# The memory's running maxima by DRAM and GpSimd, a fifth bank for the second attention's heads, the inverse sums turned a step later

## The chip, the cores and the metric

The kernel runs on one core of a Trainium2 chip. A core has five engines with a queue of their own: TensorE (PE in the rows; PEld is its weight load), VectorE (DVE), ScalarE (ACT), GpSimd (POOL) and SyncE (SP), which issues most of the DMAs. They meet only in semaphores. PE writes its products to PSUM, which has eight banks of 128 partitions x 512 floats. The metric is the device time of one execution in microseconds (us); lower is better.

## The reference, cut to what matters

Three transformer layers on 512 tokens of width 1024. The change touches the mixer of the third, in which two things run side by side: an attention of 8 heads, and a memory with matrix state (an mLSTM) of 4 heads, run forwards and backwards.

```python
# attention of the third layer, per head
s = einsum('bkgqd,bksd->bkgqs', q_blk, kt) * scale
p = softmax(s, axis=-1)
o = einsum('bkgqs,bksd->bkgqd', p, vt)

# memory, per head, chunk by chunk
d = b[..., :, None] - b[..., None, :] + ic[..., None, :]
m_t = maximum(b + m[..., None], max(where(tril, d, -inf), axis=-1))
s = einsum('bhtd,bhsd->bhts', qc, kc) * exp(d - m_t[..., None])
num = w_inter[..., None] * einsum('bhvd,bhtd->bhtv', C, qc) + einsum('bhts,bhsv->bhtv', s, vc)
h = num / maximum(abs(den), exp(-m_t))[..., None]
```

The kernel doesn't chunk the memory. It computes for each head and direction the whole 512 x 512 triangle of weights exp(a[s] - M[t]), where a is a number for each key and M a running maximum for each query, taken from the first token on (direction 0) or from the last (direction 1).

## The kernel before

**The whole.** Weights come in chunks of up to 1 MB through three buffers `raw[:, 0..2]`; ACT rounds a chunk to its high half (`wh`, L1278), DVE makes the low half (`wl`, L1906), and every large product is three PE passes. SP's `fetch(i)` may overwrite a buffer of `raw` when the low half of chunk i-3 is made. `mixed[2]` is the number of the first of the four chunks of the third layer's output weights `w_out`; they are named here +0 to +3. `mixed[2] - 1` and +2 use `raw[:, 0]`, +0 and +3 use `raw[:, 1]`, +1 uses `raw[:, 2]`.

**The stage.** On each engine the order is that of the program text. Two generators, `attend("B", ...)` and `memory()`, are advanced in turn by `side_by_side`: one step of the heads, one of the memory. The heads' first two steps come earlier, among the jobs under the last product of the input projection.

Heads: 16 units u of a head pair (j = u // 4) and a query block, each with two scores i = 2u and 2u+1. In step u PE issues the two score products of u (L848, each shown as two instructions), the transposes of the two probabilities of u-2 (L857, eight), in every fourth step `turn_inverses(j)`, one transpose of the inverse sums of the pair (L883), and for odd u-4 the output of a pair and half the queries (L873). DVE scales the scores and takes their minimum of the negated values (L2148, into one of four buffers `pl`, so only when the transpose of score i-4 has read it), forms the inverse sums (L2155), copies every second transposed probability (L2163) and the turned inverse sums (L2171). ACT takes the exponential (L1436) and copies the other transposed probabilities (L1380 into `xf`). The turned inverse sums go through DRAM (`spread`, SP's L2900 and L2907) and reach all partitions; GpSimd multiplies the pair's output with them (L2855), `DIVIDED["B"]` = 4 steps later, and ACT and DVE (L2177) make its halves.

Memory: m = 0..7 is a head and a direction; each has four cells, one for each block t of 128 keys. `Mr[d]` holds the running maxima of four heads as four rows. For each m:
- `start(m)` on PE (L1160): a product with a column of the identity, which copies row `hh` of `Mr[d]` to all 128 partitions of bank 5 (`B_MAX`). It is issued at cell 2 of m-1.
- `own(m)` on DVE (L2592): `Dd = a - M` for the four diagonal blocks, at cell 3 of m-1; it waits for the last weighing of m-2, which has read the buffer.
- `masked(m)` on GpSimd (L2863): the triangle's other side is set to a large negative number.
- ACT: the exponential of the diagonal blocks (L1770), and `decay(m, t)`, the exponential of the blocks beside the diagonal, straight from bank 5 (L1763) into one of three buffers `Db`.
- PE: `score(m, t)` (L1168) and, one m later, `outcome(m, tt)` (L1182). DVE: `weigh(m, t)` multiplies the scores with the exponentials (L2607, L2610); `divide` (L2619 to L2632) finishes the outcome.

At cell 0 of m = 3 ACT and DVE also make chunk +1 (`cur.reach`): ACT's L1278, then DVE's L1906, in the midst of their lists.

**Banks.** `banks.take(name, hold, among)` takes the bank of those in `among` whose last use was given out longest ago, and the taker waits until the engine that reads the last user's value is done. The heads use banks 0 to 3 for scores, transposes and inverse sums (`B_UNITS`) and bank 4 for the output, `M` has bank 5, scores and outcomes of the memory 6 and 7, and all but 5 once the heads are through (`B_LATE`).

**Behind the stage.** PE multiplies the attention's half with +0 (`first_column(0)`, L1216), spreads two gates (L1229), transposes the memory's output (L1237), takes +1, and then +2 and +3 (L644 on). ACT makes the high halves of +2 and +3 directly after the memory's last step, before it copies the gates.

## Time and profile before

| | us |
|---|---|
| median of 3 runs | 1911.02 |
| lowest, highest | 1909.43, 1911.91 |
| the profiled execution | 1908.34 |
| its span | 1906.6 |
| PE busy | 1848.9 (97% of the span) |
| PEld busy | 1495.3 (78%) |
| DVE busy | 1151.6 (60%) |
| ACT busy | 734.6 (39%) |
| POOL busy | 108.8 (6%) |
| mean granted clock of PE | 0.994 |

The rows further down come from one profiled execution. Its own time is 1908.34 us, of which the span between the first and the last record is 1906.6 us, so 1.7 us lie around it. The granted clock is given as a share of full speed: 1.00 is 2.4 GHz, and the lower of the two levels, 1.2 GHz, is 0.5; a stretch's number is the mean over it. "Idle before" is the time in which an engine did nothing before an instruction, with what ended it. PE's instructions overlap, so the distance from start to start is what one of them costs, and not its length.

### The profile page before, as it was taken

Reading aid. Unit: us, or ns where it says so; the run is one execution under the profiler, and the core shown is the slowest. Engines: PE = TensorE matmul, PEld = TensorE weight load, DVE = VectorE, ACT = ScalarE, POOL = GpSimd, SP = SyncE. Lnnn points to the kernel's source line nnn. Section 1 sums busy time; section 2 is a strip of 40 time slices with the busy share of each in tenths; the row PEclk is TensorE's granted clock in tenths of the full one; section 3 lists DMA queues with packets and bytes.
Section 4 is the critical chain, followed back from the end, with each engine's and each line's share of the span. In section 5 each row is a group of like instructions: output and inputs, shape, how many; then the busy total and the mean of one; then the engine's idle time right before and its main releaser. Section 6 shows DMA issues by size and latency. Waiting matters only on the chain.

```text
span 1906.6 us, 22855 instructions
## 1 busy us (share of the span) xinstructions
PE 1848.9 (97%) x9156; PEld 1495.3 (78%) x9156; DVE 1151.6 (60%) x2038; ACT 734.6 (39%) x1155; POOL 108.8 (6%) x109
## 2 busy tenths in 40 slices
PE   9999999999999999999999999899988999999997
PEld 7775888878888888878888888688655798888885
DVE  4987676555557686567554544976666554333438
ACT  4458352233233434544322222365554352222221
POOL 0341000000000152000000000000001000000000
PEclk9999999999999999999999999999999999999999
DMA  6221425433432121233434343122100313223221
GB/s 207 67 72 35 161 89 173 158 133 133 149 138 91 62 72 45 66 133 107 137 112 131 111 132 111 46 90 88 67 17 28 100 34 121 89 95 104 89 89 45
DMA packets 119018, 187.24 MB, mean 98 GB/s; under 512 B 7664, under 2 KB 72400, under 8 KB 115840
## 3 DMA queue, kind: packets, MB, share of 16 engines
q1 hardware_dynamic: 117520, 180.96, 28.9%
q0 software_dynamic: 1392, 4.82, 0.8%
q8 instruction: 72, 1.18, 0.3%
q14 instruction: 34, 0.28, 0.0%
HBM read 183.62 MB, written 2.15 MB: 97 GB/s over the span
## 4 chain that ended last, share of the span: by engine, by line
PE 77%; DVE 15%; ACT 4%; issue 3%; DMA 1%; POOL 0%; DVEq 0%; SPq 0%; ACTq 0%; POOLq 0%
PE bank L622 10%; PE bank L624 10%; PE bank L623 10%; PE bank L815 7%; PE bank L813 7%; PE bank L814 7%; PE bank L596 2%; PE bank L598 2%; PE bank L597 2%; DVE wl L1906 2%; PE bank L873 2%; DVE gb L2259 2%; PE bank L848 2%; PE bank L857 2%; DVE m L2257 1%
## 5 line engine op out<-in xcount | busy, mean ns | idle before, releaser
L1906 DVE TENSOR_TENSOR wl<-raw,wh 128x2048 fp32r<-128x2048 f32 (+1 forms) x137 | 308.2, 2254 | 190.7 <-ACT wh L1278 190.1
L1278 ACT ACTIVATE wh<-raw 128x2048 fp32r<-128x2048 f32 (+1 forms) x142 | 265.1, 1882 | 227.9 <-PE bank L815 90.4
L622 PE MATMUL bank<-xh,wh 128*128 128x512 f32 (+1 forms) x872 | 343.0, 393 | 4.0 <-DVE wl L1906 4.0
L623 PE MATMUL bank<-xh,wl 128*128 128x512 f32 (+1 forms) x872 | 342.2, 392 | 0.0
L624 PE MATMUL bank<-xl,wh 128*128 128x512 f32 (+1 forms) x872 | 342.2, 392 | 0.0
L815 PE MATMUL bank<-wh,ul 128*128 128x512 f32 x592 | 230.5, 389 | 0.0
L814 PE MATMUL bank<-wl,uh 128*128 128x512 f32 x592 | 230.4, 389 | 0.0
L813 PE MATMUL bank<-wh,uh 128*128 128x512 f32 x592 | 230.4, 389 | 0.0
L622 PEld LDWEIGHTS bank<-xh,wh 128*128 128x128 f32 (+1 forms) x872 | 163.5, 187 | 43.2 <-DVE wl L1906 5.1
L624 PEld LDWEIGHTS bank<-xl,wh 128*128 128x128 f32 (+1 forms) x872 | 163.5, 187 | 37.4
L623 PEld LDWEIGHTS bank<-xh,wl 128*128 128x128 f32 (+1 forms) x872 | 163.5, 187 | 36.7
L596 PE MATMUL bank<-wh,xh 128*128 128x512 f32 (+1 forms) x352 | 138.3, 393 | 1.7 <-DVE wl L1906 1.7
L2073 DVE TENSOR_TENSOR h<-h,bank 128x512 f32<-128x512 f32 x112 | 75.4, 683 | 105.1 <-PE bank L815 102.1
L1400 ACT ACTIVATE A<-bank 128x512 f32<-128x512 f32 x64 | 38.2, 596 | 259.0 <-PE bank L624 255.4
L598 PE MATMUL bank<-wh,xl 128*128 128x512 f32 (+1 forms) x352 | 134.1, 381 | 0.0
L597 PE MATMUL bank<-wl,xh 128*128 128x512 f32 (+1 forms) x352 | 133.9, 380 | 0.0
L814 PEld LDWEIGHTS bank<-wl,uh 128*128 128x128 f32 x592 | 111.1, 188 | 23.3
L813 PEld LDWEIGHTS bank<-wh,uh 128*128 128x128 f32 x592 | 111.2, 188 | 23.2
L815 PEld LDWEIGHTS bank<-wh,ul 128*128 128x128 f32 x592 | 111.1, 188 | 23.2
L2082 DVE TENSOR_TENSOR A<-A 128x512 f32<-128x512 f32 x64 | 44.1, 689 | 93.7 <-ACT A L1400 93.4
L1380 ACT ACTIVATE A<-bank 128x512 f32<-128x512 f32 (+4 forms) x106 | 51.4, 489 | 88.8 <-PE bank L598 32.3
L596 PEld LDWEIGHTS bank<-wh,xh 128*128 128x128 f32 x352 | 66.2, 188 | 16.6 <-issue 2.6
(352 smaller groups left out, 2962.6 us busy)
## 6 DMA issues: line engine op xcount, KB each, us to landing
raw<-in_mlp_w_up SPq DMA_DIRECT2D x32, 1024.0 KB, 5.6
raw<-in_mlp_w_down SPq DMA_DIRECT2D x32, 1024.0 KB, 5.1
raw<-in_w_ada SPq DMA_DIRECT2D x24, 1024.0 KB, 5.0
raw<-in_b_w_in SPq DMA_DIRECT2D x12, 1024.0 KB, 5.3
raw<-in_w_gate SPq DMA_DIRECT2D x11, 1024.0 KB, 5.3
raw<-in_w_up SPq DMA_DIRECT2D x11, 1024.0 KB, 5.5
raw<-in_w_in SPq DMA_DIRECT2D x10, 1024.0 KB, 5.1
raw<-in_w_down SPq DMA_DIRECT2D x10, 1024.0 KB, 5.0
```

What stands on the lines that cost most here:

```text
L596: pe.matmul(o, X, H[:, k, :], start=kk == 0, stop=False)
L597: pe.matmul(o, X, L[:, k, :], start=False, stop=False)
L598: step = pe.matmul(o, Y, H[:, k, :], start=False, stop=kk == 7)
L622: pe.matmul(o, H[:, k, c], xh[:, k, :], start=k == 0, stop=False)
L623: pe.matmul(o, L[:, k, c], xh[:, k, :], start=False, stop=False)
L624: step = pe.matmul(o, H[:, k, c], xl[:, k, :], start=False, stop=k == 7)
L813: pe.matmul(o, X, H[:, f, :], start=f == 0, stop=False)
L814: pe.matmul(o, X, L[:, f, :], start=False, stop=False)
L815: step = pe.matmul(o, Y, H[:, f, :], start=False, stop=f == nf - 1)
L1278: act.activation(slots[slot_of[i]][0][:, 0:n], raw[:, i % NRAW, 0:n], ACT.Copy).then_inc(*s_high.up(i))
L1906: dve.tensor_tensor(L[:, 0:n], raw[:, i % NRAW, 0:n], H[:, 0:n].bitcast(F), ALU.subtract).then_inc(*s_low.up(i))
L2073: dve.tensor_tensor(hv, hv, ps, ALU.add).then_inc(*s_row.up(name))
```

## The change

- `start(m)` is gone, and with it `M`'s bank. SP writes `Mr[0]` and `Mr[1]` to a DRAM tensor `rows_m` and loads row (d, hh) from there to all 128 partitions of one of four buffers `Mb`, which lie in `raw[:, 0]`. The first four are loaded once the low half of chunk `mixed[2] - 1` is made, m = 4 + j behind the spreading of the inverse sums of pair j, when ACT and GpSimd have read m - 4.
- `raw[:, 0]` is thus taken until ACT and GpSimd have read the last maxima. Chunk +2 is fetched only then, and +3 and the chunks behind it after +2, in SP's order. Before, +2 was issued as soon as `raw[:, 0]` was free, ahead of the stage, and +3 at 1356.4 us.
- DVE's `own(m)` is gone. GpSimd subtracts M from a itself, directly ahead of the selection, at cell 2 of m-1 instead of 3, and waits there for the maxima's transfer and the last weighing of m-2.
- ACT's `decay` reads `Mb` and waits for the transfer, not for DVE.
- `B_UNITS` is (0, 1, 2, 3, 5). When the heads are through the memory takes any bank.
- `INVERTED = {"A": 0, "B": 1}`: the inverse sums of the heads "B" are transposed and copied one step later. The attention of the first layer ("A") stays as it is.

```diff
-        B_UNITS, B_OUT, B_MAX, B_MEM, B_LATE, ANY = range(4), (4,), (5,), (6, 7), (0, 1, 2, 3, 4, 6, 7), range(8)
+        B_UNITS, B_OUT, B_MEM, ANY = (0, 1, 2, 3, 5), (4,), (6, 7), range(8)
+        INVERTED = {"A": 0, "B": 1}
+        Mb = [raw[:, 0, 512 * i:512 * i + 512] for i in range(4)]
+        def maxima(m):
+            return s_maxima[m % 4], 16 * (m // 4 + 1)
+        def maxima_read(m):
+            return s_act.at(("Db", m, T - 2 if MEM[m][1] == 0 else T - 1))
...
-                        if g % T == T - 1:
-                            turn_inverses(g // T)
+                    g = u - lag - INVERTED[key]
+                    if 0 <= g < N and g % T == T - 1:
+                        turn_inverses(g // T)
...
-                def start(m):
-                    hh, d = MEM[m]
-                    b = banks.take(("M", m), False, B_MAX)
-                    sel = ident[32 * d:32 * d + 4, 32 * d + hh:32 * d + hh + 1].broadcast_to([4, P])
-                    w.wait_ge(*banks.free(("M", m), s_act.sem))
-                    w.wait_ge(*s_step.at(("Mr", d)))
-                    pe.matmul(bank[b][:, :], sel, Mr[d], start=True, stop=True).then_inc(*s_mm.up(("M", m)))
...
-                    w.wait_ge(*s_step.at(("D", m)))
+                    w.wait_ge(*maxima(m))
                     w.wait_ge(*s_act.at(("ecol", 1)))
-                    act.activation(Db[n % 3][:, 0:o1 - o0], bank[banks.of["M", m]][:, o0:o1], ACT.Exp, bias=acol[:, d, t, hh:hh + 1],
+                    act.activation(Db[n % 3][:, 0:o1 - o0], Mb[m % 4][:, o0:o1], ACT.Exp, bias=acol[:, d, t, hh:hh + 1],
...
-                def own(m):
-                    hh, d = MEM[m]
-                    M = bank[banks.of["M", m]][:, :].rearrange("p (t q) -> p t q", t=T)
-                    w.wait_ge(*s_mm.at(("M", m)))
-                    w.wait_ge(*s_act.at(("ecol", 1)))
-                    if m > 1:
-                        w.wait_ge(*s_step.at(("ST", m - 2, T - 1)))
-                    dve.scalar_tensor_tensor(Dd[m % 2], M, -1.0, acol[:, d, :, hh].unsqueeze(2).broadcast_to([P, T, P]), ALU.mult,
-                                             ALU.add).then_inc(*s_step.up(("D", m)))
...
-                    w.wait_ge(*s_step.at(("D", m)))
+                    hh, d = MEM[m]
+                    w.wait_ge(*maxima(m))
+                    w.wait_ge(*s_act.at(("ecol", 1)))
+                    w.wait_ge(*(s_step.at(("ST", m - 2, T - 1)) if m > 1 else s_step.at(("conv", 7))))
+                    pool.tensor_tensor(Dd[m % 2], acol[:, d, :, hh].unsqueeze(2).broadcast_to([P, T, P]),
+                                       Mb[m % 4].rearrange("p (t q) -> p t q", t=T), ALU.subtract).then_inc(*s_pool.up(("own", m)))
+                    w.wait_ge(*s_pool.at(("own", m)))
...
-                        if m + 1 < len(MEM) and t == 3:
+                        if m + 1 < len(MEM) and t == 2:
                             masked(m + 1)
...
+            def spread_maxima(m):
+                hh, d = MEM[m]
+                if m > 3:
+                    w.wait_ge(*maxima_read(m - 4))
+                    w.wait_ge(*s_pool.at(("own", m - 4)))
+                sp.dma_start(Mb[m % 4], rows_m[d, hh].partition_broadcast(P)).then_inc(s_maxima[m % 4], 16)
...
-                if i == mixed[2] + 3:
+                if i == mixed[2] + 1:
+                    for d in range(2):
+                        w.wait_ge(*s_step.at(("Mr", d)))
+                        sp.dma_start(rows_m[d], Mr[d]).then_inc(s_rows, 16)
+                    w.wait_ge(s_rows, 32)
+                    w.wait_ge(*low_of(mixed[2] - 1))
+                    for m in range(4):
+                        spread_maxima(m)
                     for j in range(4):
                         spread("B", j)
+                        spread_maxima(4 + j)
+                    w.wait_ge(*maxima_read(len(MEM) - 1))
+                    w.wait_ge(*s_pool.at(("own", len(MEM) - 1)))
```

**The order on PE, steps u = 5 and 6.** Before; the list begins in step 5 with the transposes (L857), and goes on with inverse sums, output, a product of the memory, the maxima of m = 1 and the scores of step 6:

```order
L857 MATMUL bank1<-C,pl 128x128 [waits s_step]
L857 MATMUL bank1<-C,pl 128x128 x3
L883 MATMUL bank3<-C,att 8x128 [waits s_step]
L873 MATMUL bank4<-xf,A 64x256 x8
L1168 MATMUL bank7<-A 128x256
L1160 MATMUL bank5<-A,C 128x512 [waits s_act]
L848 MATMUL bank0<-A 128x512 [waits s_act,s_step]
L848 MATMUL bank2<-A 128x512
```

Now (L872, L888, L1176, L863, L898 are the lines L857, L873, L1168, L848, L883 of before):

```order
L872 MATMUL bank3<-C,pl 128x128 [waits s_act]
L872 MATMUL bank3<-C,pl 128x128 x3
L888 MATMUL bank4<-xf,A 64x256 x8
L1176 MATMUL bank7<-A 128x256
L863 MATMUL bank5<-A 128x512 [waits s_step]
L863 MATMUL bank0<-A 128x512
L872 MATMUL bank2<-C,pl 128x128 [waits s_step]
L872 MATMUL bank2<-C,pl 128x128 x3
L872 MATMUL bank1<-C,pl 128x128 [waits s_act]
L872 MATMUL bank1<-C,pl 128x128 x3
L898 MATMUL bank3<-C,att 8x128 [waits s_step]
```

The maxima's product is gone, and the inverse sums stand behind the transposes of step 6, in a bank that no score of the step has.

**The order on PE, the last head pair, steps u = 16 to 18.** Before, from the last transposes on:

```order
L857 MATMUL bank0<-C,pl 128x128 x3
L857 MATMUL bank2<-C,pl 128x128 x4
L883 MATMUL bank1<-C,att 8x128 [waits s_step,s_act]
L873 MATMUL bank4<-xf,A 64x256 x8
L1168 MATMUL bank6<-A 128x384 [waits s_step]
L1182 MATMUL bank7<-A,xf 128x130 x7
L1160 MATMUL bank5<-A,C 128x512 [waits s_act]
```

Now:

```order
L872 MATMUL bank5<-C,pl 128x128 x3
L872 MATMUL bank0<-C,pl 128x128 [waits s_act]
L872 MATMUL bank0<-C,pl 128x128 x3
L888 MATMUL bank4<-xf,A 64x256 [waits s_act]
L888 MATMUL bank4<-xf,A 64x256 x7
L1176 MATMUL bank6<-A 128x384 [waits s_step]
L1190 MATMUL bank7<-A,xf 128x130 x7
L898 MATMUL bank2<-C,att 8x128
```

The output (L888, before L873) stands ahead of the inverse sums (L898, before L883), which come after the outcome of the memory (L1190, before L1182).

**The order on GpSimd, from the first maxima on.** Before, from the masks of m = 0 and 1 to that of m = 4 (L2855 is the heads' division, L2863 the selection):

```order
L2863 AFFINE_SELECT rz<-rz 128x512 [waits s_step] x2
L2855 TENSOR_TENSOR pl<-pl,A 128x512 [waits s_inv_b0,s_act]
L2863 AFFINE_SELECT rz<-rz 128x512 [waits s_step]
L2855 TENSOR_TENSOR pl<-pl,A 128x512 [waits s_inv_b1,s_act]
L2863 AFFINE_SELECT rz<-rz 128x512 [waits s_step]
L2855 TENSOR_TENSOR pl<-pl,A 128x512 [waits s_inv_b0,s_act]
L2863 AFFINE_SELECT rz<-rz 128x512 [waits s_step]
```

Now (L2847 is the division, L2857 the subtraction, L2860 the selection):

```order
L2857 TENSOR_TENSOR rz<-acol,raw 128x512 [waits s_step,s_act,s_maxima0]
L2860 AFFINE_SELECT rz<-rz 128x512 [waits s_pool]
L2857 TENSOR_TENSOR rz<-acol,raw 128x512 [waits s_maxima1]
L2860 AFFINE_SELECT rz<-rz 128x512 [waits s_pool]
L2847 TENSOR_TENSOR pl<-pl,A 128x512 [waits s_inv_b0,s_act]
L2857 TENSOR_TENSOR rz<-acol,raw 128x512 [waits s_step,s_maxima2]
L2860 AFFINE_SELECT rz<-rz 128x512 [waits s_pool]
L2847 TENSOR_TENSOR pl<-pl,A 128x512 [waits s_inv_b1,s_act]
L2857 TENSOR_TENSOR rz<-acol,raw 128x512 [waits s_step,s_maxima3]
L2860 AFFINE_SELECT rz<-rz 128x512 [waits s_pool]
```

Each selection has a subtraction ahead of it, which is what waits for the maxima's transfer and for DVE.

## Rows read from the trace of the kernel before

**Rows 1.** Windows: start:end, length, busy of each engine, granted clock, DMA share, GB/s
```profile
1366.00:1434.26 68.26, 60.44 (x360) 34.88 (x358) 42.15 (x120) 39.15 (x103) 6.36 (x7) 1.00 0.05 13
...
1438.33:1445.70 7.37, 7.37 (x33) 4.50 (x33) 3.65 (x12) 0.00 (x0) 0.00 (x0) 0.59 0.25 52
```

**Rows 2.** Groups by form, 1360 to 1485: shape, count, busy us, mean ns, idle
```profile
L1160 PE MATMUL bank<-A,C 4*128 4x512 f32 x16 | 9.0, 639 | 0.0
...
L2592 DVE SCALAR_TENSOR_TENSOR rz<-bank,acol 128x512 f32<-128x512 f32 x8 | 5.5, 684 | 3.0 <-PE bank L1160 3.0
...
L2855 POOL TENSOR_TENSOR pl<-pl,A 128x512 f32<-128x512 f32 x4 | 5.1, 1272 | 13.4 <-ACT pl L1380 13.4
...
L2863 POOL TENSOR_SCALAR_AFFINE_SELECT rz<-rz 128x512 f32<-128x512 f32 x8 | 5.1, 634 | 202.3 <-DVE rz L2592 202.3
...
L2607 DVE SCALAR_TENSOR_TENSOR xf<-bank,rz 128x384 f32<-128x384 f32 x4 | 2.2, 552 | 1.4 <-PE bank L1168 1.3
```

**Rows 3.** PE in order of time: start, us, line, count, idle before
```profile
1364.60 1.13 PE L848 MATMUL bank<-A 64*128 64x512 f32 x4 [0.93 <-ACT ecol L1670]
...
1368.02 1.13 PE L848 MATMUL bank<-A 64*128 64x512 f32 x4 [0.21 <-DVE pl L2148]
...
1378.16 0.27 PE L883 MATMUL bank<-C,att 128*8 128x128 f32 x1 [0.50 <-DVE pl L2148]
1378.36 1.95 PE L873 MATMUL bank<-xf,A 128*64 128x256 f32 x16
...
1385.34 1.13 PE L848 MATMUL bank<-A 64*128 64x512 f32 x4 [1.04 <-DVE pl L2148]
...
1398.96 0.91 PE L1168 MATMUL bank<-A 128*128 128x384 f32 x2
...
1401.37 1.12 PE L1160 MATMUL bank<-A,C 4*128 4x512 f32 x2
1402.42 1.13 PE L848 MATMUL bank<-A 64*128 64x512 f32 x4
```

**Rows 4.** DVE, then ACT, in order of time, inside one round
```profile
1384.44 0.75 DVE L2148 TENSOR_SCALAR_CACHE_REDUCE pl<-bank,q_rms 128x512 f32<-128x512 f32 x1
...
1385.98 0.57 ACT L1380 ACTIVATE xf<-bank 128x512 f32<-128x512 f32 x1
```

**Rows 5.** DVE, then PE, in order of time, around the stop of PE
```profile
1435.78 2.29 DVE L1906 TENSOR_TENSOR wl<-raw,wh 128x2048 fp32r<-128x2048 f32 x1 [4.05 <-ACT wh L1278]
...
1439.44 0.61 DVE L2629 TENSOR_SCALAR A<-bank,den 128x128 f32<-128x128 f32 x2
...
1438.33 0.37 PE L883 MATMUL bank<-C,att 128*8 128x128 f32 x1 [4.08 <-DVE att L2155]
...
1447.81 1.95 PE L873 MATMUL bank<-xf,A 128*64 128x256 f32 x16
```

**Rows 6.** GpSimd, DVE, then PE, in order of time, behind 1450
```profile
1450.48 1.27 POOL L2855 TENSOR_TENSOR pl<-pl,A 128x512 f32<-128x512 f32 x1 [2.15 <-ACT pl L1380]
...
1450.85 0.56 DVE L2607 SCALAR_TENSOR_TENSOR xf<-bank,rz 128x384 f32<-128x384 f32 x1 [1.26 <-PE bank L1168]
...
1454.91 0.68 DVE L2177 TENSOR_TENSOR ul<-pl,uh 128x512 fp32r<-128x512 f32 x1
...
1456.44 0.94 PE L1182 MATMUL bank<-A,xf 128*128 128x130 f32 x6 [0.62 <-DVE xf L2610]
...
1468.73 0.91 PE L1182 MATMUL bank<-A,xf 128*128 128x130 f32 x6 [0.43 <-DVE den L2619]
```

**Rows 7.** Landing times of L2893's loads, 1300 to 1500; then ACT in order of time
```profile
DMA to landing us min/median/max: 4.9/5.2/7.0
...
1471.39 0.57 ACT L1763 ACTIVATE C<-bank,acol 128x384 f32<-128x384 f32 x1
...
1478.63 3.71 ACT L1278 ACTIVATE wh<-raw 128x2048 fp32r<-128x2048 f32 x2
```

**Rows 8.** GpSimd's line L2836: duration ns min/median/max, first and last start
```profile
L2836 POOL TENSOR_TENSOR A<-A x28: 613/668/2693, 661.3 to 732.8; 128x256 f32<-128x256 f32 x28
```

16 lines of the change are left out of this document (6 added, 10 removed).

## The prediction

> **What bounds the kernel now.** The page first: PE is busy for 97% of the span and holds 77% of the chain that ended last, so time is won only where PE stands still, does work that can go, or runs at its lower clock. The diff touches one stage, so the next view is the windows over it [rows 1]. From 1366 to 1434.26 us PE is busy for 60.44 of 68.26 us, then stands still until 1438.33 (4.08 us, L883's wait [rows 5]), then runs for 7.37 us at a mean granted clock of 0.59. Outside this stage the instruction lists are the same, so whatever is gained or lost here should arrive at the end unchanged, if the weights of the next stage are there in time. I call a round what both generators issue for one yield: one score unit u of the attention heads (two L848 products), the transposes of unit u-2, sometimes L883 and L873, then one cell of the memory. L848 of u=2 stands at 1364.60.
>
> **Why PE waits in a round.** L848 of u=2 starts at 1364.60 and that of u=3 at 1368.02, 3.42 us later [rows 3]; the L848 at 1385.34 waits for DVE's L2148 of the round before, 1.04 us. The reason is the rotation. A round takes four banks out of four, so the next two scores land in the two banks that L2148 has yet to read, and L2148 is two instructions of 0.75 us each [rows 4]; they overlap a little, and I count 0.67 for each. They cannot start before the round's own first transposes, whose buffer they overwrite. With a fifth bank the order of the changed kernel shows scores in the bank freed a round earlier and in that of the round's first score: the wait ends with the first L2148, 0.67 us earlier. In a round with L883, L883 takes the fifth bank, the next scores get the same two banks again, and nothing is won: so u=3, 4, 5, 9 and 13 win, 7, 11 and 15 don't. The transposes behind them still need ACT's copy of the round before (L1380 at 1385.98, 0.57 us, in order behind two exponentials) [rows 4], which gives part of it back.
>
> **The sum, part by part.**
> 1. L848 at 1364.60 waited 0.93 us for ACT's ecol, whose bank it took [rows 3]. Its banks are now others. **0.9 us.**
> 2. u=3 to 5 and the first L883. L883 at 1378.16 idles 0.50 us [rows 3] because its bank is that of the score just issued; with its own issue (0.2, from L883 at 1378.16 to the L873 at 1378.36) that is 0.7. In the changed kernel it stands a round later, in a round that ends in a wait, and its bank is long free. Three bank waits of 0.67 are 2.0 more, of which I take 1.8 since two of them meet ACT's copy. **2.5 us.**
> 3. u=9 and 13 with the L883 of their rounds: 0.67 + 0.7 each, less what the second transposes wait for ACT, a few hundredths. **2.6 us.**
> 4. L1160, the product that spread a row of maxima over the partitions: 16 instructions (two to a product), 9.0 us busy [rows 2], 1.05 us from its start to the instruction behind it (1401.37 to the L848 at 1402.42) [rows 3]. That for m=0 lies inside the 3.42 us of a round that waits anyway: nothing. Those for m=1 to 4 lie in stretches where PE never waits: 4 x 1.05. **4.2 us.**
> 5. The hole at 1434.26. DVE's L1906 waits 4.05 us for ACT's wh and runs 2.29 us; only then come the reciprocal and L883 [rows 5]. In the changed kernel L883 is behind the next memory products, and L873 (16 instructions, 1.95 us at full clock [rows 3]) runs at once, to 1436.2 in the old times. But then the product of cell (3,2) needs the bank that L2629 empties behind that same L1906, until 1439.44 + 0.61 = 1440.05 [rows 5]. So PE stands still for 3.9 us in place of 4.08, only later. I expect the clock to fall as before. It cost (1 - 0.59) x 7.37 = 3.0 us [rows 1]. From 1440.1 there follow a product of 384 columns with 14 instructions of L1182 (2.41 us, as from 1398.96 to 1401.37 [rows 3]), one of 512 columns (1.05, as L1160), L883 (0.2) and 3.0 us for the clock: 1446.8, against 1447.8 for the same L873 before [rows 5]. That 1.0 us is L1160 of m=4, counted above. **0.0 us** of its own; 3.0 if the clock doesn't fall.
> 6. From 1450 on only the memory is left. The three L1160 for m=5 to 7 go (3.15 us). What is late next there: before m=5, DVE's L2177 and L2592 stand ahead of the weighing for which L1182 waits 0.62 us [rows 6]; without L2592 (0.68 [rows 2]) that chain is shorter by 0.6, and 0.5 is won. Before m=6 PE has no wait and wins the whole 1.05, before m=7 the chain through L2592 (wait of 0.43 [rows 6]) shortens too and 0.9 is won. **2.5 us.**
>
> Sum: 0.9 + 2.5 + 2.6 + 4.2 + 0.0 + 2.5 = **12.7 us.** The profiled execution would fall from 1908.34 to 1895.6 us (span 1906.6 to 1893.9). The median of the runs is 2.68 us above the profiled one, so 1911.02 becomes **1898.3 us**.
>
> **What I cost at nothing, and its cover.**
> - GpSimd's subtraction. The trace has no such instruction at this stage; the nearest is L2855, same shape, both inputs in SBUF, 1272 ns; the longest row of a two-input GpSimd instruction with a broadcast input is L2836 with 2693 ns for half the elements, so 1.3 to 5.4 us [rows 2, 8]. I take 1.3, since 2693 is two of 28 and the median of that line is 668 ns for half the size. With the selection (634 ns [rows 2]) and ACT's exponential (0.6, taken from its copy of the same size [rows 4]) a head's own blocks take 2.5 us from the last weighing of the head before last. It has four cells for that: L1182 of two heads lie 1468.73 - 1456.44 = 12.29 us apart with two L1160 in it [rows 6], so (12.29 - 2.1) / 2 = 5.1 us a head when only the memory runs. Cover: 2.6 us; what is beyond it costs three times, at m=5 to 7.
> - The Trainium skill (GPSIMD Engine Reference, 4.1 Engine selection) speaks against this step: elementwise work on two inputs belongs to VectorE, GpSimd being about half as fast. The rows agree, 1272 against 684 ns [rows 2]. By that rule the stage would lose 8 x 0.6 = 4.7 us; by the rows it loses none, since GpSimd stands still and DVE's 684 ns lie on the way to the weighing.
> - ACT reads the maxima from SBUF instead of PSUM, and waits for their transfer instead of DVE. No row shows a broadcast of that size; the loads of 1 MB land within 7.0 us [rows 7], and each row of maxima is loaded two turns or more ahead. Queued behind SP's new waits are only transfers that are due later.
> - The third and fourth chunk of w_out. They are now issued when the last Db is made (before: 1471.39 + 0.57) and 1 MB lands 5.2 us later, at 1477.2 [rows 7]. ACT converts it at 1478.63 [rows 7], after the memory in either kernel. Cover: 1.4 us; beyond it ACT's later copies are late first.
> - The inverse sums of the last head pair start some 6 us later (L883 behind 1445 in the old times in place of 1438.33), so their division, which ran at 1450.48 [rows 6], may slip by 1 us. The subtraction for m=5 stands behind it in GpSimd's queue and has the cover above.
>
> **The rivals.**
> - *The clock holds.* The hole is now behind 1.9 us of PE work and may fall otherwise against whatever lowers the clock. For it: two short stops instead of one. Against: 3.9 us is as long as the stop that did it. 12.7 + 3.0 = 15.7: **1895.3 us.** Chance 0.13.
> - *Another engine takes the place of the banks.* ACT's copy and DVE's in-order queue then pace the rounds. For: the copy already ends a PE wait now, and DVE holds cells, copies and maxima in one queue. Against: DVE is busy for 42.15 and ACT for 39.15 of the 68.26 us [rows 1]. Terms 2, 3 and half of 6 go: 12.7 - 2.5 - 2.6 - 1.2 = 6.4: **1904.6 us** (1902 to 1907). Chance 0.20.
> - *It doesn't do what it says*: the rotation gives PE the same waits and L1160 fell into gaps. Against: the order, and L1160 and the L848 behind it follow without a wait [rows 3]. **1911.0 us.** Chance 0.05.
> - *Slower: GpSimd holds up DVE.* Place: all eight subtractions. If DVE stood still while GpSimd works, each turn would cost 1.27 + 0.63 us, 15.2 in all and 2.5 more than is won; at 2.69 + 0.63 per turn 26.6, so **1924.9 us**. It decides against the change from 12.7 / 8 = 1.6 us a turn, and by over 0.2% from 2.1. Against it: while L2855 ran from 1450.48 to 1451.75, DVE's L2607 took 0.56 us, and its mean is 552 ns [rows 2, 6]. The Trainium skill (GPSIMD Engine Reference, 1. Specifications) says that GpSimd shares its SBUF interfaces with VectorE and that instructions with two SBUF inputs contend; L2607 has one input in PSUM, so the row does not refute it for others. Chance 0.07, with whatever else costs.
>
> **The numbers.** Forecast 1898.3 (1896 to 1901) with 0.55. The range takes in the clock's rival below and two thirds of the second above: 1894.5 to 1905.5. A measurement here tells 0.2% (3.8 us) from no change. Faster by more: 0.55 + 0.13 + 0.19 = 0.87; within: 0.07; slower: 0.06.
>
> **What the profile of the changed kernel would show.** L1160's product and DVE's L2592 gone, about nine tenths of their 9 us missing from PE's work; L848 to L848 2.8 to 3.1 us at u=3 and 9 but 3.4 at u=7; no wait before the L883 product; the hole behind the first L873 of the last pair, near 3.9 us, and a granted clock near 0.6 behind it; GpSimd's subtraction near 1.3 us and never a long wait of ACT on GpSimd; the last two w_out loads issued some 4 us before the memory ends, with no new PE wait after them. I would be wrong if ACT waits for GpSimd or DMA in most turns, if DVE's instructions lengthen, or if the stop before the second conversion grows.

## The result, and the profile after

| | before | after |
|---|---|---|
| median of 6 runs each, us | 1909.68 | 1898.22 |
| lowest, highest | 1909.20, 1911.91 | 1893.56, 1901.48 |
| the profiled execution, its span | 1908.34, 1906.6 | 1897.57, 1895.8 |

The ratio is 0.9936, 95% interval 0.9925 to 0.9946. In the rows of after the lines have moved: L848 is L863, L857 L872, L873 L888, L883 L898, L1168 L1176, L1182 L1190, L1216 L1221; DVE's L2148 is L2152, L2177 L2182, L2610 L2605, L2619 L2614, L2629 L2624, L1906 L1910; ACT's L1278 is L1283, L1380 L1385, L1763 L1768; GpSimd's L2855 is L2847, L2863 L2860, and L2857 is the new subtraction. The first part of the page of after:

```profile
span 1895.8 us, 22838 instructions
## 1 busy us (share of the span) xinstructions
PE 1842.3 (97%) x9140; PEld 1495.4 (79%) x9140; DVE 1144.5 (60%) x2030; ACT 735.0 (39%) x1155; POOL 116.2 (6%) x117
```

PE is busy for 6.6 us less (before 1848.9), DVE for 7.1 less. To see where 10.8 us of span went I cut both traces at two instructions that both have: the first score of u=1, and the first product behind the memory (L1216, now L1221). Before they stand at 1359.59 and 1476.24, after at 1363.16 and 1465.48. So the **stretch** between them went from 116.65 to 102.32 us, 14.33 less. Behind it nothing changed (430.4 and 430.3 us to the end). Ahead of it, where the instruction lists of PE are the same, 3.57 us were lost. Windows (length, busy of PE, PEld, DVE, ACT and POOL, granted clock, DMA share, GB/s) say to what. Of before:

```profile
640.00:650.00 10.00, 10.00 (x44) 7.97 (x43) 9.86 (x9) 6.97 (x5) 0.00 (x0) 1.00 0.34 109
1236.00:1246.00 10.00, 7.54 (x27) 6.01 (x28) 6.41 (x23) 6.24 (x14) 1.07 (x2) 0.83 0.10 7
```

and of after, with the two windows that answer [rows 1]:

```profile
640.00:650.00 10.00, 10.00 (x30) 6.93 (x29) 9.01 (x8) 5.90 (x4) 0.00 (x0) 0.70 0.33 107
1238.00:1248.00 10.00, 7.47 (x22) 5.82 (x21) 6.79 (x23) 6.63 (x15) 1.07 (x2) 0.66 0.10 7
1365.00:1430.79 65.79, 61.52 (x383) 36.75 (x381) 41.20 (x121) 43.56 (x113) 12.06 (x13) 1.00 0.08 25
1434.39:1441.00 6.61, 6.61 (x35) 4.71 (x35) 3.41 (x11) 1.20 (x3) 0.00 (x0) 0.74 0.01 3
```

In 640 to 650 the clock was at its lower level for part of the time, in before it was not; the window ahead (630 to 640) was at 0.96. Together that is 3.4 us of clock, and from 674 on the same PE instructions stand 2.4 us later than in before. The other 1.2 us came between 1220 and 1250: near 1240 both kernels fell to the lower level, before for 1.7 us of clock and after for 3.4. In all, the profile of after lost 10.2 us to the clock while PE had work, and that of before 6.8. In the rounds PE is now busy for 61.52 of 65.79 us, 93.5%, where it was 60.44 of 68.26, 88.5% [rows 1]. The loss to the clock behind the hole is (1 - 0.74) x 6.61 = 1.7 us, where it was 3.0 over the window of [rows 1] and 3.4 in all.

PE in order of time, the rows that answer [rows 3] and the hole of [rows 5]:

```profile
1363.16 1.13 PE L863 MATMUL bank<-A 64*128 64x512 f32 x4
...
1367.17 1.13 PE L863 MATMUL bank<-A 64*128 64x512 f32 x4
...
1369.92 1.13 PE L863 MATMUL bank<-A 64*128 64x512 f32 x4 [0.59 <-DVE pl L2152]
...
1383.08 0.27 PE L898 MATMUL bank<-C,att 128*8 128x128 f32 x1
...
1384.51 1.13 PE L863 MATMUL bank<-A 64*128 64x512 f32 x4 [0.93 <-DVE pl L2152]
...
1389.77 1.13 PE L863 MATMUL bank<-A 64*128 64x512 f32 x4
...
1392.42 1.13 PE L863 MATMUL bank<-A 64*128 64x512 f32 x4
...
1421.40 1.13 PE L863 MATMUL bank<-A 64*128 64x512 f32 x4 [0.93 <-DVE pl L2152]
...
1434.39 1.50 PE L1176 MATMUL bank<-A 128*128 128x384 f32 x2 [3.60 <-DVE A L2624]
```

u=2 no longer waits for ecol. u=3 follows u=2 by 2.75 us (before 3.42), u=9 follows u=8 by 2.65 (3.42), and u=7 follows u=6, at 1381.09, by 3.42 as before, with 0.93 us of waiting: that is the round in which L898 took the fifth bank. No L898 waits. The hole is still there, now in front of a memory product. DVE in it:

```profile
1430.06 2.29 DVE L1910 TENSOR_TENSOR wl<-raw,wh 128x2048 fp32r<-128x2048 f32 x1 [3.68 <-ACT wh L1283]
```

The new instruction and its neighbours, by form, 1355 to 1475 (count, busy us, mean ns, idle before):

```profile
L2857 POOL TENSOR_TENSOR rz<-acol,raw 128x512 f32<-128x512 f32 x8 | 8.4, 1048 | 126.8 <-ACT ecol L1675 122.5 <-DVE den L2614 4.3
...
L2860 POOL TENSOR_SCALAR_AFFINE_SELECT rz<-rz 128x512 f32<-128x512 f32 x8 | 5.1, 635 | 1.2 <-POOL rz L2857 0.2
L1774 ACT ACTIVATE rz<-rz 128x512 f32<-128x512 f32 x8 | 4.9, 616 | 0.1
```

GpSimd subtracts in 1.05 us, and ACT, which takes the exponential of its result, waited 0.1 us for it in eight turns.

### The profile page after: what moved, and what is told of

The parts are those of the page before. It is cut to its first block, busy times and chain, and to the rows that moved or that the text cites. A ratio compares the mean times of both kernels' runs of the same rounds, so it can differ in the third digit from the quotient of the medians.

```text
span 1895.8 us, 22838 instructions
## 1 busy us (share of the span) xinstructions
PE 1842.3 (97%) x9140; PEld 1495.4 (79%) x9140; DVE 1144.5 (60%) x2030; ACT 735.0 (39%) x1155; POOL 116.2 (6%) x117
## 4 chain that ended last, share of the span: by engine, by line
PE 78%; DVE 15%; ACT 4%; issue 3%; POOL 0%; DMA 0%; DVEq 0%; ACTq 0%
PE bank L637 10%; PE bank L638 10%; PE bank L639 10%; PE bank L830 7%; PE bank L829 7%; PE bank L828 7%; PE bank L611 2%; PE bank L613 2%; PE bank L612 2%; DVE wl L1910 2%; PE bank L888 2%; PE bank L863 2%; DVE gb L2264 2%; PE bank L872 2%; DVE m L2262 1%
## 5 line engine op out<-in xcount | busy, mean ns | idle before, releaser
L1910 DVE TENSOR_TENSOR wl<-raw,wh 128x2048 fp32r<-128x2048 f32 (+1 forms) x137 | 307.9, 2251 | 192.6 <-ACT wh L1283 192.0
L1283 ACT ACTIVATE wh<-raw 128x2048 fp32r<-128x2048 f32 (+1 forms) x142 | 265.2, 1882 | 228.9 <-PE bank L830 90.5
L2086 DVE TENSOR_TENSOR A<-A 128x512 f32<-128x512 f32 x64 | 44.1, 689 | 93.7 <-ACT A L1405 93.5
L1385 ACT ACTIVATE A<-bank 128x512 f32<-128x512 f32 (+4 forms) x106 | 51.5, 490 | 90.3 <-PE bank L613 32.3
```

The source lines that it names most:

```text
L1283: act.activation(slots[slot_of[i]][0][:, 0:n], raw[:, i % NRAW, 0:n], ACT.Copy).then_inc(*s_high.up(i))
L1910: dve.tensor_tensor(L[:, 0:n], raw[:, i % NRAW, 0:n], H[:, 0:n].bitcast(F), ALU.subtract).then_inc(*s_low.up(i))
```

## How the runs below are read

A stretch of 102 us in a program of 1900 can be read far more finely than the total. Each kernel's trace is cut at the same instructions: the scores of u=1, 2, 6 and 15 and the first L1221. Beside the last part stands what the clock took in the stretch: the sum of (1 - granted clock) x length over windows of 1 us. All numbers in us.

| kernel | median (lowest to highest, runs) | ratio to before, 95% | u=1 to 2 | 2 to 6 | 6 to 15 | 15 to L1221 | clock's part |
|---|---|---|---|---|---|---|---|
| before | 1909.68 (1909.20 to 1911.91, 6) | | 5.01 | 17.32 | 44.83 | 49.49 | 3.4 |
| after | 1898.22 (1893.56 to 1901.48, 6) | 0.9936 (0.9925 to 0.9946) | 4.01 | 13.92 | 40.31 | 44.08 | 1.7 |
| a_same | 1893.37 (1892.67 to 1898.00, 4) | 0.9914 (0.9901 to 0.9928) | 4.01 | 13.92 | 40.32 | 44.27 | 1.7 |
| a_same2 | 1898.02 (1895.51 to 1901.15, 5) | 0.9935 (0.9922 to 0.9947) | 4.01 | 13.92 | 40.30 | 46.93 | 5.1 |
| a_maxonly | 1901.68 (1900.03 to 1902.27, 5) | 0.9950 (0.9938 to 0.9962) | 5.01 | 16.25 | 42.73 | 41.98 | 0 |
| a_inv0 | 1895.63 (1892.88 to 1897.93, 5) | 0.9926 (0.9912 to 0.9939) | 4.01 | 14.03 | 38.90 | 45.17 | 3.4 |
| a_4banks | 1907.69 (1905.28 to 1908.77, 11) | 0.9980 (0.9971 to 0.9989) | 5.01 | 15.47 | 44.84 | 45.72 | 3.4 |
| b_inv1 | 1914.41 (1910.65 to 1916.38, 10) | 1.0014 (1.0005 to 1.0023) | 5.01 | 16.55 | 46.94 | 53.20 | 8.5 |
| a_noreach | 1894.16 (1889.10 to 1894.55, 4) | 0.9907 (0.9893 to 0.9921) | 4.01 | 13.92 | 40.31 | 38.32 | 0 |
| a_nr_inv0 | 1888.89 (1888.55 to 1891.26, 4) | 0.9888 (0.9875 to 0.9902) | 4.01 | 14.03 | 38.89 | 38.64 | 0 |
| a_lowlate | 1896.08 (1894.02 to 1897.97, 5) | 0.9926 (0.9913 to 0.9940) | 4.01 | 13.92 | 40.31 | 44.27 | 3.4 |
| a_latefetch | 1895.98 (1893.83 to 1898.52, 5) | 0.9923 (0.9910 to 0.9937) | 4.01 | 13.92 | 40.31 | 45.36 | 3.4 |
| a_dvesub | 1900.07 (1899.61 to 1901.92, 5) | 0.9945 (0.9933 to 0.9958) | 4.01 | 14.40 | 40.31 | 48.31 | 5.1 |
| a_sub3 | 1898.83 (1896.71 to 1901.55, 5) | 0.9939 (0.9927 to 0.9952) | 4.01 | 14.21 | 40.32 | 44.77 | 1.7 |

The rounds repeat to 0.02 us in three profiles of one kernel (after, a_same, a_same2); the last part and the total don't, since the clock falls there or not. Even less the clock's part the stretch of this one kernel still moved between 100.0 and 100.8, so that a smaller difference in the last part shows nothing. The start of the stretch, behind the same PE instructions in all, lay between 1358.66 and 1363.77. Each ratio is to the kernel before as it ran beside that run, at medians from 1909.68 to 1911.92.

## The experiments

**The changed kernel again, twice (a_same, a_same2).** No edit.

> The changed kernel again, unaltered. In its profile the stage (second score product of the heads to the memory's end) took 102.3 us against 116.6 before, 14.3 less, yet the whole only 10.8 less: between 640 and 650 us, long before the stage, PE ran at a granted clock of 0.70 where the kernel before had 1.00, which cost 3.6 us. Theory: such a fall comes in some executions and has nothing to do with the change; the time spreads from 1894 to 1901 us again, 0.6% below before, and each execution's mean clock goes with its time (0.994 with the short ones, 0.991 with the long ones). Rival: the spread arises in the stage itself, at the stop of PE; then the stage in this profile is longer or shorter than 102.3 by some us and the stretch at 640 us is at 1.00.

> The changed kernel again, word for word, as the yardstick for the other three runs of this group, and a test of what repeats: from the first score of the second pair (u=1) to the first product after the memory it took 102.32 and 102.52 us in two profiles. Theory: what is queued repeats, so this stretch less the clock's loss in it (1.7 in both) comes out at 100.6 to 100.8 again, the hole before L1176 at 3.60, and what differs from run to run is only how much of the 1.2 GHz level the stretch gets. Rival: the work itself shifts from run to run, and the stretch less its clock loss moves by over 0.5 us. Median 1893 to 1898.

The three medians of one kernel, 1898.22, 1893.37 and 1898.02, differ by 4.9 us. Both sides of the first question were partly right: in a_same the fall near 640 was absent and the stretch took 102.52 us, as the theory has it, but in a_same2 the fall was there and the stretch took 105.16, so the spread arises in both places. In the stretch mainly the clock moved, apart from one wait of 1.7 to 2.2 us in front of L1190 (below). Granted clock of two windows of a_same2:

```profile
1432.00:1439.00 7.00, 5.67 (x19) 4.34 (x19) 3.16 (x11) 0.96 (x3) 0.00 (x0) 0.51 0.01 2
1449.00:1453.00 4.00, 4.00 (x18) 3.30 (x17) 1.93 (x9) 1.87 (x7) 0.79 (x2) 0.57 0.00 0
```

After the hole of 3.59 us PE ran at the 1.2 GHz level almost to 1439, and again from 1449, behind a wait of 1.86 us. In the trace of after the same hole (3.60) was followed by 3.4 us at that level and no second fall. The stretch less the clock's part is 100.6, 100.8 and 100.0: the 0.5 us that the rival names were just passed. Perhaps a lowered clock hides some of the waits; no run tests that.

**The first part alone: maxima by DRAM and GpSimd (a_maxonly).**

```diff
-        B_UNITS, B_OUT, B_MEM, ANY = (0, 1, 2, 3, 5), (4,), (6, 7), range(8)
+        B_UNITS, B_OUT, B_MEM, ANY = (0, 1, 2, 3), (4,), (6, 7), range(8)
...
-        INVERTED = {"A": 0, "B": 1}
+        INVERTED = {"A": 0, "B": 0}
```

> The first part of the change alone: the maxima go through DRAM and GpSimd subtracts them, but the heads keep four banks and the inverse sums are turned in their old step. Theory of the prediction's terms: the four maxima products (4.2 us), the memory-only part (2.5) and most of the banks' waits go (the fifth bank by itself 2 to 4 us): 1902 us against 1911 of before. Rival, after the run with four banks that came out 8.5 us behind in the stage: the rotation of four banks hangs on DVE's releases, so the PE time that the four products leave comes back as waits; the rounds from u=6 to u=15 stay within 1 us of the 44.8 of before less at most 2.1, and the time is 1904 to 1908. Rounds shorter by 2.1 and time 1902 speak for the first, rounds of 44 or more for the second. The clock's loss in the stage (3.4 us in before) is read apart.

1901.68: the first theory. The round parts give back the products that stood in them and nothing else: 17.32 to 16.25 (1.07, one L1160) and 44.83 to 42.73 (2.10, two). The last part without the clock falls from 46.1 to 42.0, which is the fourth L1160, the memory-only part, and a hole of 3.52 in place of 4.08 us. The clock didn't fall in the stretch of this execution at all, though a hole of 3.5 us was there:

```profile
1436.92 0.27 PE L898 MATMUL bank<-C,att 128*8 128x128 f32 x1 [3.52 <-DVE att L2159]
```

```profile
1360.00:1480.00 120.00, 103.82 (x630) 69.59 (x629) 74.38 (x240) 65.53 (x179) 18.91 (x21) 1.00 0.17 54
```

**The inverse sums in their old step, with all else changed (a_inv0), and the later step alone, on the kernel before (b_inv1).** The edit of a_inv0 is the second of the two above; b_inv1 has it in the other direction in the kernel before (`g = u - lag - 1` for pass B's `turn_inverses` and its reader on DVE).

> The changed kernel with the inverse sums transposed in the old step (0 in place of 1). With a fifth bank the transpose no longer waits for a score's bank, so the first three cost at most 0.3 us each. The last stands again behind the reciprocal that waits for the second conversion, and the output product behind it: the stop is as long as before (4.1 us) and 1.9 us of work comes after it instead of ahead. Expected: 2 to 3 us more than the changed kernel, 1900 to 1901. If also the clock's fall behind the stop is that of before (3.0 us, against 1.7 in the changed kernel): 4 us, 1902. Rival: 0, because the memory's product behind it waits for the same conversion.

> The kernel before with nothing but the inverse sums one step later (four banks, maxima by product, DVE subtracts). By the sum L883's waits of 0.5 us in three rounds go, but with four banks it takes the bank of a score of its own round and shifts the rotation, so 0 to 1.5 us; at the stop the output product (1.9 us) moves ahead of it and the cell's product then waits: 0.2 to 2 us, more if the clock's fall shrinks. Expected 1 to 3 us below the kernel before, 1907 to 1909. Rival: it is this part that won the 1.3 us of clock seen in the profile, then 4 us, 1906.

Both came out against me. The later step makes the rounds *longer*: 44.83 to 46.94 with four banks, and 38.90 (a_inv0) to 40.3 (after) with five. With the old step L898 stands in the round of u=5 and the score of u=7 waits 0.37 us; with the later one L898 stands in the round of u=6, takes the bank that u=7 would have had, and u=7 waits 0.93. In the old step the 1.95 us of the output (L888) follow L898 in the same round and cover the bank that it takes: u=6 doesn't wait in either kernel. The round of u=6 has no output. PE of a_inv0, then of a_same, in order of time:

```profile
1376.70 1.13 PE L863 MATMUL bank<-A 64*128 64x512 f32 x4
1377.76 1.09 PE L872 MATMUL bank<-C,pl 128*128 128x128 f32 x8
1378.69 0.39 PE L1176 MATMUL bank<-A 128*128 128x128 f32 x2
1379.45 1.13 PE L863 MATMUL bank<-A 64*128 64x512 f32 x4 [0.37 <-DVE pl L2152]
```

```profile
1376.80 1.13 PE L863 MATMUL bank<-A 64*128 64x512 f32 x4
1377.86 1.09 PE L872 MATMUL bank<-C,pl 128*128 128x128 f32 x8
1378.79 0.27 PE L898 MATMUL bank<-C,att 128*8 128x128 f32 x1
1378.90 0.39 PE L1176 MATMUL bank<-A 128*128 128x128 f32 x2
1380.22 1.13 PE L863 MATMUL bank<-A 64*128 64x512 f32 x4 [0.93 <-DVE pl L2152]
```

2.75 us from score to score against 3.42 at u=7, and 0.48 and 0.76 at u=11 and 15: 1.91, of which 0.49 is won elsewhere. The hole of a_inv0 was 3.86 us. Less the clock its stretch is 98.7 us, 1.3 to 2.1 less than that of the changed kernel, so the third part of the change works against the other two. The medians of a_inv0 and the changed kernel can't be told apart. b_inv1 has a median 2.5 us above that of before on the same chip (1911.92), more than the two parts of its rounds (1.3 us). In its profile the clock lost 8.5 us in the stretch where before lost 3.4; less the clock the stretch is 113.2 us in both, so that its last part gives back what the rounds lose.

```profile
1442.00:1456.00 14.00, 13.01 (x39) 7.03 (x40) 5.16 (x17) 2.04 (x5) 0.63 (x1) 0.51 0.18 52
```

**Four banks with the rest of the change (a_4banks).** The first of the two edits above.

> The changed kernel with four banks for the heads, 0 to 3, bank 5 left unused until the heads are through. By my sum the bank waits come back at u = 3, 4, 5, 9 and 13, 0.67 us each less what ACT's copy covers: about 3 us more than the changed kernel, near 1901. L863 of u=3 stands 3.4 us behind that of u=2 again (2.75 with five banks). Rival (other engines pace the rounds): less than 1 us, 1898 to 1899, since DVE or ACT would end the waits anyway.

1907.69, 6.7 us beyond what was expected. The later step and the fifth bank depend on each other: with four banks and the later step the rounds are as long as before the change (44.84), though two L1160 have gone from them. Three scores that waited 0.40 to 1.04 us for DVE now wait longer, for the ACT copy whose bank they get:

```profile
1386.16 1.13 PE L863 MATMUL bank<-A 64*128 64x512 f32 x4 [1.63 <-ACT xf L1385]
...
1405.98 1.13 PE L863 MATMUL bank<-A 64*128 64x512 f32 x4 [0.99 <-ACT xf L1385]
...
1426.22 1.13 PE L863 MATMUL bank<-A 64*128 64x512 f32 x4 [1.63 <-ACT xf L1385]
```

So the bank is worth 1.00 + 2.22 + 3.83 = 7.05 us of the round parts where the inverse sums keep their old step (a_maxonly to a_inv0), and 1.00 + 1.55 + 4.52 = 7.07 where they don't (a_4banks to a_same). The fifth bank on the kernel before, where the maxima hold bank 5, wasn't tried, so what it is worth beside L1160 isn't shown.

**Without the early conversion (a_noreach).**

```diff
-                        if m == 3 and t == 0:
-                            cur.reach(high, 2)
...
-                        if m == 3 and t == 0:
-                            cur.reach(low, 2)
```

> The changed kernel without the early conversion of the first prefetched w_out chunk: ACT's and DVE's halves of it (the 1.9 us and 2.25 us conversions at m=3) no longer stand in front of the last head's work. Theory: the hole of 3.6 us before the row L1176 at 1434.39 is DVE waiting 3.68 us for that chunk's ACT half; it closes to under 0.6, and the clock's loss behind it (1.7) goes too: 4 to 5.3 us less than the changed kernel, minus what the chunk costs at the memory's end, at most 1 us: 1889 to 1894 where the changed kernel makes 1893.4 to 1898. Rival: the conversion is only moved to the end of the memory, where ACT idles 5.3 us but DVE then is late by its 2.25 us and the next projection waits for it: gain 1.5 us or none.

The last part falls from 42.6 (a_same, less the clock) to 38.3, the hole is gone and the clock stays up. Nothing is paid for it later: from L1190 at 1442.75 to L1221 at 1460.33 it takes 17.58 us, the same as in a_same (1443.81 to 1461.39), and from L1221 to the end 432.1 us, which is 430.4 without a fall of 1.7 near 1862, as in before and after. PE where the hole was:

```profile
1429.46 1.95 PE L888 MATMUL bank<-xf,A 128*64 128x256 f32 x16
1431.33 0.91 PE L1176 MATMUL bank<-A 128*128 128x384 f32 x2
1432.08 1.73 PE L1190 MATMUL bank<-A,xf 128*128 128x130 f32 x14
```

In the median less of it is seen, 1894.16 (just above the 1889 to 1894 expected) against 1893.4 to 1898.2 for the changed kernel: outside the stretch this profile lost 8.5 us to the clock while PE had work, that of a_same 3.4.

**Both (a_nr_inv0).** The edits of a_noreach and a_inv0.

> The changed kernel without the early conversion of the w_out chunk and with the inverse sums of pass B turned in their old step. Theory: with five banks the old step makes the rounds from u=6 to u=15 shorter (38.9 us against 40.3), and without the conversion no hole opens: the stretch from u=1 to the memory's end comes to 96.6 - 1.4 = 95.1 us with no clock loss in it, and the time to 1.4 us under that of the changed kernel without the conversion: 1888 to 1893. Rival: the later turn was there so that the last division does not stand in front of TensorE, and a wait of 1 to 1.5 us before L898 or L888 at the end of the rounds takes it back: stretch 96.5, the same time as without the conversion alone.

1888.89 us, ratio 0.9888 (0.9875 to 0.9902): the fastest kernel, 9.1 us under a_same2 on the same chip, and faster than both kernels of the case. The stretch is 95.57 us and the clock stays at 1.00 in it. It is 1.0 shorter than in a_noreach, of 1.4 expected: the rounds give 1.42, the last part takes 0.3 back and u=2 to 6 takes 0.1. The medians of the two are 5.3 us apart, on different chips; what the other 4 us are isn't shown.

```profile
1360.00:1480.00 120.00, 113.83 (x692) 77.99 (x691) 80.21 (x243) 69.79 (x184) 18.92 (x21) 1.00 0.20 65
```

**DVE's half of the conversion later (a_lowlate).**

```diff
-                        if m == 3 and t == 0:
+                        if m == 4 and t == 2:
                             cur.reach(low, 2)
```

> The changed kernel with DVE's half of the early conversion (2.25 us, and the 3.68 us for which DVE stands waiting for ACT's half) moved six scores later, ACT's half left in its place. It tells apart which of the two halves opens the hole of 3.60 us before L1176. If it is DVE's place: the hole falls to what ACT's 1.9 us alone leave, 0 to 1 us, the stretch from u=1 to the memory's end to 97 to 98.5 us, time 3 to 5 us under the changed kernel. If it is ACT's place: the hole stays over 2 us and the time within 1.5 us.

The first for the hole, neither for the time. The hole at L1176 is gone, so it was DVE's place that made it, not ACT's 1.9 us. But in the new place DVE's 2.28 us stand on the way to a weighing, and a hole of 4.27 us opens there. The stretch less the clock is 99.1 us, 0.9 to 1.7 less than that of the changed kernel. DVE, then PE:

```profile
1438.15 2.28 DVE L1910 TENSOR_TENSOR wl<-raw,wh 128x2048 fp32r<-128x2048 f32 x1
1440.35 0.68 DVE L2182 TENSOR_TENSOR ul<-pl,uh 128x512 fp32r<-128x512 f32 x1
1440.95 0.28 DVE L2605 SCALAR_TENSOR_TENSOR xf<-bank,rz 128x128 f32<-128x128 f32 x1
...
1441.29 1.67 PE L1190 MATMUL bank<-A,xf 128*128 128x130 f32 x6 [4.27 <-DVE xf L2605]
```

**The w_out chunks fetched later (a_latefetch).**

```diff
                     w.wait_ge(*s_pool.at(("own", len(MEM) - 1)))
+                    w.wait_ge(*s_mm.at(("hm", len(MEM) - 1, 1)))
```

> The changed kernel with the third and fourth w_out chunk fetched later: the queue also waits for the last product of the memory, some 4.5 us. Theory: ACT idles 5.3 us ahead of its conversion at 1477.55 and the chunk that is latest waits 0.5 us now, so the 4.5 us are hidden: within 0.5 us of the changed kernel. Rival (the prediction's sentence that beyond a cover of 1.4 us ACT's later copies are late first): 4.5 less 1.4 show up at the first projection after the memory: 3 us more, with a TensorE wait for ACT or DVE there.

Within the changed kernel's scatter, with no new TensorE wait behind the memory, and 430.2 us from L1221 to the end less the clock (430.3 in after): the first theory. The loads are issued 0.3 us behind L1221 instead of 4.5 ahead of it; ACT waits 3.05 and 0.77 us for them and still idles 1.91 us afterwards. The cover isn't the 1.4 us of the prediction. In the trace of after ACT already waits for the second of the two chunks, and then stands idle for 5.3 us until its next copy:

```profile
1470.32 1.93 ACT L1283 ACTIVATE wh<-raw 128x2048 fp32r<-128x2048 f32 x1 [0.54 <-DMA raw<-in_w_out]
1477.55 0.60 ACT L1385 ACTIVATE A<-bank 128x512 f32<-128x512 f32 x1 [5.30 <-PE bank L1234]
```

**DVE subtracts in GpSimd's place (a_dvesub).**

```diff
-                    pool.tensor_tensor(Dd[m % 2], acol[...].broadcast_to([P, T, P]), Mb[m % 4]..., ALU.subtract)
+                    dve.scalar_tensor_tensor(Dd[m % 2], Mb[m % 4]..., -1.0, acol[...].broadcast_to([P, T, P]), ALU.mult, ALU.add)
```

> The changed kernel, but DVE takes the maxima (from the same loaded rows) off the columns, eight operations of 128 x 512, and GpSimd keeps only the selection. Theory 1, that GpSimd's share of the change matters little since it was never what was late: DVE's eight operations of about 0.6 us lie in its idle time except in the memory-only part, where DVE feeds TensorE: 0.5 to 2 us slower than the changed kernel. Theory 2, that DVE's queue paces the rounds: each of the four subtractions inside the rounds delays a release by 0.6 and four in the memory-only part too: 4 to 5 us slower.

DVE takes 676 ns for each. The stretch less the clock is 101.9 us, 1.1 to 1.9 more than that of the changed kernel: 0.48 in u=2 to 6, the hole 4.20 in place of 3.60, and a wait of 1.28 in front of an L1190 where 0.68 was. That is theory 1; the median of 1900.07, 1.9 to 6.7 above the changed kernel's, has the clock in it too (5.1 us in the stretch).

**GpSimd's subtraction three times (a_sub3).**

```diff
+                    for _ in range(2):
+                        pool.tensor_tensor(Dd[m % 2], ...the same operands..., ALU.subtract)
+                        # and a wait for it
```

> The changed kernel with GpSimd's subtraction issued three times for each head (8 x 2 x 1.05 us more on GpSimd, the same values). The prediction gave the subtraction a cover of 2.6 us on the way to the next weighting. Theory: 2.1 us more per head fit into it: within 1 us of the changed kernel, no longer ACT wait for GpSimd inside the rounds. Rival 1: the cover is smaller in the memory-only part, where the heads follow each other faster: four heads by up to 2.1, 2 to 6 us slower. Rival 2, the slower case of the prediction: DVE's operations with two SBUF operands stretch while GpSimd works (one took 1.13 us in place of 0.68): twice as much GpSimd work beside them costs 1 to 2 us without any wait for GpSimd.

0.8 us above a_same2 in the median, and the stretch less the clock is 101.6, 0.8 to 1.6 above the changed kernel. So most of the 2.1 us a head fit in, as the theory says, but each rival holds in part. In the memory-only part ACT waited 2.04 and 0.62 us for GpSimd, and L1190 waited 0.39 and 0.88 us where it had waited 0 and 0.68: that fits the first, though DVE was held there too (L2614 took 0.80 and 0.69 us). And one of the added subtractions ran for 2.97 us beside DVE's conversion, which took 2.51 us in place of 2.29 and made the hole 3.82: this is what the second rival asks. GpSimd, then DVE:

```profile
1425.11 2.17 POOL L2858 TENSOR_TENSOR rz<-acol,raw 128x512 f32<-128x512 f32 x2
1427.36 2.97 POOL L2861 TENSOR_TENSOR rz<-acol,raw 128x512 f32<-128x512 f32 x1
...
1426.92 2.51 DVE L1910 TENSOR_TENSOR wl<-raw,wh 128x2048 fp32r<-128x2048 f32 x1 [3.67 <-ACT wh L1283]
```

The subtraction began beside DVE's conversion and ended 0.90 us behind its end (1430.33 and 1429.43): as if it had stood still while DVE read two operands from SBUF, and had then done most of its own 1.05 us.

## What DVE and GpSimd do to each other

The same in the other direction in a_same, in front of the first weighing of m=5. GpSimd, DVE, PE:

```profile
1439.43 1.27 POOL L2847 TENSOR_TENSOR pl<-pl,A 128x512 f32<-128x512 f32 x1 [13.63 <-DMA A<-sums]
1440.65 1.05 POOL L2857 TENSOR_TENSOR rz<-acol,raw 128x512 f32<-128x512 f32 x1
...
1440.70 1.02 DVE L2614 TENSOR_TENSOR den<-den,ecol 128x2 f32<-128x2 f32 x1
...
1443.81 0.94 PE L1190 MATMUL bank<-A,xf 128*128 128x130 f32 x6 [2.15 <-DVE xf L2605]
```

L2614 works on two numbers per partition, both operands in SBUF, and takes 0.15 us elsewhere. Here it took 1.02 and ended with GpSimd's subtraction (1441.72 and 1441.70). The kernels can be laid side by side: by how much the DVE instruction beside GpSimd's work was stretched, and how long L1190 then waited. In after it is L2182, beside the selection at 1446.47, in the others L2614 beside the subtraction.

| | stretched, us | wait before L1190, us | less 1.28 |
|---|---|---|---|
| a_maxonly, a_inv0, a_noreach, a_nr_inv0 | none there | 1.27, 1.28, 1.28, 1.28 | 0 |
| a_sub3 | 0.46 - 0.15 = 0.31 | 1.58 | 0.30 |
| a_latefetch | 0.54 - 0.15 = 0.39 | 1.67 | 0.39 |
| after (L2182) | 1.13 - 0.68 = 0.45 | 1.72 | 0.44 |
| a_same2 | 0.74 - 0.15 = 0.59 | 1.86 | 0.58 |
| a_4banks | 0.97 - 0.15 = 0.82 | 2.10 | 0.82 |
| a_same | 1.02 - 0.15 = 0.87 | 2.15 | 0.87 |

The wait grows by the stretch, to 0.01 us. (a_lowlate and a_dvesub are left out: in front of this L1190 the one has the conversion, the other DVE's own subtraction.) GpSimd is there at that moment because its L2847, ahead of the subtraction in its queue, waited for the spread inverse sums, which the later step makes late (first row above). In a_inv0 it is through in time; GpSimd, then DVE:

```profile
1439.05 1.05 POOL L2857 TENSOR_TENSOR rz<-acol,raw 128x512 f32<-128x512 f32 x1
...
1440.94 0.15 DVE L2614 TENSOR_TENSOR den<-den,ecol 128x2 f32<-128x2 f32 x1
```

So the mechanism of the prediction's slower rival exists. Its price here is 0.4 to 0.9 us in one place of the program, not 15. Beside the other seven subtractions of after and a_same no DVE instruction of L2182 or L2614 was held. In a_noreach and a_nr_inv0 L2614 was held at m=4 (0.67 and 0.93 us) with no wait of PE behind it, in a_noreach twice more (0.39 and 0.23 us), again without one. L2602, with an operand in PSUM, takes 552 ns for 384 columns as before [rows 2]. The Trainium skill (SBUF — State Buffer, Who interferes with whom) says just this: a DVE instruction with two SBUF inputs contends with a GpSimd instruction that reads SBUF, one with at most one SBUF input and outside the two-port modes doesn't, and the order of issue decides who is blocked. The rows agree that either can be the one held: in a_same GpSimd began first (1440.65 and 1440.70) and DVE was held, in a_sub3 DVE began first (1426.92 and 1427.36) and GpSimd was. In a_noreach the selection took 1.19 us in place of 0.63 beside an undisturbed L2182, though by the recorded starts it was 0.02 us ahead; starts that close don't settle the order.

## The prediction, point by point

The forecast was 1898.3 us and the median is 1898.22. Part of that is luck: medians of the same kernel lay between 1893.4 and 1898.2. The stretch is the fairer judge, and it went from 116.65 - 3.41 = 113.24 us without the clock's part to 102.32 - 1.70 = 100.62, 12.6 less where the sum said 12.7.

1. *u=2's wait, 0.9.* 5.01 to 4.01: 1.00.
2. *u=3 to 5 and the first L883, 2.5.* 17.32 to 13.92 is 3.40, less one L1160 (1.05): 2.35.
3. *u=9 and 13, 2.6.* 44.83 to 40.31 is 4.52, less 2.10: 2.42. The sum of 2 and 3 is right (4.8 for 5.1), its reason isn't, and that the two errors cancel is luck. The sum had 3.0 us for the bank's waits and 2.1 for three L883, whose own 0.7 us I took as won because each moves into a round that waits anyway. The runs show the opposite sign: in the same rounds the bank alone gives 6.05 us (7.05 with u=2's wait), and the later step takes 1.3 of it back, because L898 there takes the bank that would have ended the wait. That u=7, 11 and 15 win nothing was itself a price of the third part, and I wrote it down as a given.
4. *L1160, 4.2.* a_maxonly gives 1.07 and 2.10 for the three in the rounds. That for m=0 was in fact free.
5. *The hole, 0.0, and 3.0 if the clock holds.* The hole was 3.60, forecast 3.9. For the clock I had one row of before and carried it over as if it repeated. It doesn't: in after, a_same and a_same2, the same instructions behind the same hole, it took 1.7, 1.7 and 5.1 us, and in a_maxonly nothing behind 3.52 us. The term is a range from 0 to some 5 us, and no hole longer or shorter by a few tenths decides it.
6. *The memory-only part, 2.5.* From the second L873 of the last pair to L1216 it was 28.43 (1447.81 to 1476.24), and from the second L888 to L1221 26.05 (1439.43 to 1465.48): 2.38. Its pieces: 0.15 before m=5 (forecast 0.5) and 2.2 behind it (1.95). What the first lacks is GpSimd's hold on L2182 (0.45).

*What was costed at nothing.* The subtraction took 1.05, not 1.3 us, and ACT did not wait for it; before, ACT had waited 5.8 us in six turns for the selection behind DVE's L2592. The rows of maxima, 256 KB each on arrival, landed 3.5 to 5.0 us after their issue (median 3.7), long ahead. The w_out loads went out at 1460.95, 4.5 us before the memory's end, and landed later than estimated; ACT waited 0.54 us for one, hidden by 5.3 us of idling. The sentence that ACT's copies are late first beyond a cover of 1.4 us was wrong: a_latefetch delays the loads by about 4.9 us at no cost that can be measured. The inverse sums' division did slip, and the subtraction behind it with it: ACT waited 0.86 us for the division (L2847) and no engine for the subtraction, but GpSimd then held DVE (0.4 to 0.9 us, above).

*The rivals.* That the clock holds was half true in one profile and untrue in another. That ACT's copies take the place of the banks holds for 0.22 to 0.32 us in four rounds (the second half of L872), 1.0 us in all; in a_4banks ACT's copies do pace three scores. That the change does nothing is refuted by the rows. *Slower* is answered above: in after and a_same DVE was held once, not in all eight turns.

One piece was missing from the list: the falls ahead of the stage, near 640 and 1240 us. The profiled executions of before and after ran the same PE instructions there, and after came out 3.6 us later. Had I compared the two spans alone (10.8 us, where the sum said 12.7), I would have put 1.9 us on the wrong terms. The expectation of a_same, which puts 3.6 us on the fall near 640 alone, is wrong by the same 1.2 us.
